# Low parts written over the loaded weight tiles, and loads that wait for TensorE

## The reference

```
for layer in range(2):
    mx, mc = silu(c) @ w_mod[layer] + b_mod[layer], silu(c_ctx) @ w_mod[layer] + b_mod[layer]
    hx, hc = modulate(rmsnorm(x), mx), modulate(rmsnorm(ctx), mc)
    # layer 0: GLA heads and SSD heads, scanned both ways;  layer 1: bidirectional mLSTM
    f = features(h @ w_in)
    x = x + mx[2] * (f @ w_out)
    x = x + mx[5] * ((silu(h @ w1) * (h @ w3)) @ w2)        # h normed and modulated again
return rmsnorm(x)
```

## Time and profile before

| what | us |
|---|---|
| median of 3 runs | 2714.57 (2714.4 to 2721.69) |
| profiled execution, its own time | 2722.84 |
| span of the profiled execution | 2721.1 |
| TensorE busy | 2430.7 |
| VectorE busy | 1483.2 |
| GpSimd busy | 1090.8 |
| mean granted clock of TensorE | 0.934 of full |

### The profile page before, as it was taken

How to read it: one execution, slowest core, us unless ns; L and a number is a source line. 1 busy time by engine, 2 the same in 40 slices (tenths; PEclk the granted TensorE clock), 3 DMA queues, 4 the chain that set the end, 5 groups by cost and what they waited for, 6 DMA issues and landing times.

```text
span 2721.1 us, 33407 instructions
## 1 busy us (share of the span) xinstructions
PE 2430.7 (89%) x11967; PEld 1896.6 (70%) x11967; DVE 1483.2 (55%) x2465; ACT 640.8 (24%) x1041; POOL 1090.8 (40%) x822
## 2 busy tenths in 40 slices
PE   6999999988568899999999898797877968899997
PEld 2878888877226788888888687655444636788886
DVE  3695668683676468877876456203465264322223
ACT  2203434533773311000000321102212021210001
POOL 2443334413672244434354454233000402666663
PEclk9999999989778899999999899898987979899998
DMA  6853334335240124344444254263122211233331
GB/s 241 246 163 105 103 109 129 108 125 165 84 115 24 47 78 124 109 113 119 112 121 102 62 144 154 105 218 119 57 72 78 62 43 39 85 93 100 93 91 49
DMA packets 392114, 292.90 MB, mean 108 GB/s; under 512 B 31330, under 2 KB 351260, under 8 KB 391996
## 3 DMA queue, kind: packets, MB, share of 16 engines
q1 hardware_dynamic: 333452, 201.22, 25.5%
q10 hardware_dynamic: 58544, 90.10, 9.7%
HBM read 249.50 MB, written 41.78 MB: 107 GB/s over the span
## 4 chain that ended last, share of the span: by engine, by line
PE 54%; DVE 10%; ACT 3%; issue 2%; DMA 1%; ACTq 1%; DVEq 0%
PE PS L800 41%; PE PS L1288 3%; DVE xcr L2003 2%; PE PS L1258 2%; PE PS L1195 2%; ACT nh L1366 1%; PE PS L1221 1%; PE PS L752 1%; DVE xcr L1998 1%; PE PS L746 1%; PE PS L1234 1%; PE PS L809 1%; ACT xcr L1698 1%; DVE mf_acc L1905 0%; DVE mtmp L2456 0%
## 5 line engine op out<-in xcount | busy, mean ns | idle before, releaser
L640 POOL TENSOR_TENSOR w_hi<-w_raw,ones 128x128 fp32r<-128x128 f32 x244 | 150.8, 618 | 1303.8 <-PE PS L800 796.9
L800 PE MATMUL PS<-act_hi,w_hi 128*128 128x512 f32 (+1 forms) x2080 | 642.3, 367 | 32.1 <-DVE act_lo L1962 18.3
L800 PE MATMUL PS<-act_lo,w_hi 128*128 128x512 f32 (+1 forms) x2080 | 624.9, 358 | 0.0
L800 PE MATMUL PS<-act_hi,w_lo 128*128 128x512 f32 (+1 forms) x2080 | 624.8, 358 | 0.0
L643 POOL TENSOR_TENSOR w_lo<-w_raw,w_hi 128x1024 fp32r<-128x1024 f32 (+1 forms) x244 | 598.0, 2451 | 20.4
L800 PEld LDWEIGHTS PS<-act_hi,w_hi 128*128 128x128 f32 x2080 | 345.7, 192 | 94.3 <-issue 31.4
L800 PEld LDWEIGHTS PS<-act_lo,w_hi 128*128 128x128 f32 x2080 | 345.9, 192 | 58.2 <-issue 0.5
L800 PEld LDWEIGHTS PS<-act_hi,w_lo 128*128 128x128 f32 x2080 | 345.1, 191 | 58.9
L1905 DVE SCALAR_TENSOR_TENSOR mf_acc<-mf_ring,cs,mf_acc 128x128 f32<-128x128 f32 x784 | 280.6, 433 | 2.0
L641 POOL TENSOR_SCALAR w_hi<-w_raw 128x896 fp32r<-128x896 f32 (+1 forms) x244 | 245.1, 1004 | 0.0
L2184 DVE SCALAR_TENSOR_TENSOR xT<-PS,modv,xT 128x512 f32<-128x512 f32 (+1 forms) x120 | 75.0, 658 | 266.6 <-PE PS L800 266.5
(11 more groups left out here) (322 smaller groups left out, 3256.4 us busy)
## 6 DMA issues: line engine op xcount, KB each, us to landing
w_raw<-in_ffn_w SPq DMA_DIRECT2D x120, 512.0 KB, 3.9
mf_ring<-in_w_mod SPq DMA_DIRECT2D x56, 512.0 KB, 4.0
w_raw<-in_a_w_in SPq DMA_DIRECT2D x44, 512.0 KB, 5.6
proj<-stage ACTq DMA_DIRECT2D x44, 384.0 KB, 2.7
w_raw<-in_b_w_up SPq DMA_DIRECT2D x32, 512.0 KB, 4.0
m_ring<-in_w_mod SPq DMA_DIRECT2D x12, 1024.0 KB, 9.1
rows<-g_d SPq DMA_DIRECT2D x16, 768.0 KB, 5.0
m_raw<-in_w_mod SPq DMA_DIRECT2D x4, 2048.0 KB, 17.1
```

Source lines behind the costliest of these rows:

```text
L640: pool.tensor_tensor(w_hi[:, s, 0], w_raw[:, s, 0], ones[:], ALU.mult)
L800: last = pe.matmul(slot(s)[:, c0:c1], w[:, s, k, :], x[:, k, c0:c1], start=k == 0 and w is w_hi and x is hi, stop=k == kt - 1 and w is w_lo)
```

## The change

The tile `w_lo` is placed at the address of `w_raw`, so that the subtraction writes over its own input, and 16 KB of each partition are free. A slot can then be loaded only when TensorE has finished the unit in it: the loads wait for `mm_done` where they waited for `w_split`. In the SSD stretch the fourth load of out1 would wait for out0's last unit; it moves behind the rows of head 2.

```
+        w_raw_at = top[0]
         w_raw = sb("w_raw", [P, RING, KD, P])
         w_hi = sb("w_hi", [P, RING, KD, P], F32R)
-        w_lo = sb("w_lo", [P, RING, KD, P], F32R)
+        w_lo = nc.alloc_sbuf_tensor_at("w_lo", [P, RING, KD, P], F32R, offset=w_raw_at)
...
                 def load(r, s, kt=kt, src=src):
-                    sp.wait_ge(w_split, r * RING + (s - RING + 1))
+                    sp.wait_ge(mm_done, r * RING + (s - RING + 1))
                     sp.dma_start(w_raw[:, s, 0:kt], src(r, s)).then_inc(w_in[s], 16)
...
-                        sp.wait_ge(w_split, n - RING + 1)
+                        sp.wait_ge(mm_done, n - RING + 1)
                         sp.dma_start(w_raw[:, n % RING], wk[:, :, col:col + P]).then_inc(w_in[n % RING], 16)
...
                     sp.dma_start(rdiag[:], proj0[C0 + 1]).then_inc(b1_in, 16)
-                    each_ring(sp, n0, RING, load)
+                    for s in range(RING - 1):
+                        load(n0 // RING, s)
                     sp.wait_ge(cb_mm, 6)
                     sp.dma_start(bct[:, 0], proj0[B0 + 1]).then_inc(b1_in, 16)
                     for h in range(2, SSD_HEADS):
                         sp.wait_ge(exp_done, h - 1)
                         load_rows(h)
+                        if h == 2:
+                            load(n0 // RING, RING - 1)
```

## The result

Median 2746.06 us (2743.04 to 2750.84, 4 runs) against 2716.56 us before (2714.4 to 2721.69, 4 runs): ratio 1.0107, 95% interval 1.0085 to 1.0130. The change costs 29 us; the forecast had 2724 with a range to 2738. The runs of the kernel before that were made beside the experiments are more in number and have higher medians, 2717 to 2721 us (single runs from 2710 to 2728).

What follows compares the result with a forecast made beforehand. TensorE, busy for 89% of the span, was taken as the bound, so only its waits count. Terms 8.4 + 2.7 - 4 + 4 - 3 + 0.8 + 0.5 = +9.4 us, laid on the median 2714.57, gave 2724.0 us; range 2706 to 2738.

Steps and rivals of the forecast that it cites:

- what is queued behind the wait on SP: qkv's start: m_ring's first load issued about 30 us later, so TensorE stalls for modulation sums; +8.4 us, bounds +2.3 and +15.
- In place: GpSimd's subtraction writing over its own first input: no cost taken.
- the steady state: Most units: a tile is ready 7.8 us after unit n-4 ends, wanted at 16.3, leaving 8.5 us; no cost.
- The lock elsewhere in qkv: Later splits in qkv relieve the products behind the 5.6 us wait at L834; -4 us, bounds -7.8 and 0.
- Layer 0's feed-forward: Splits against products: up00's start +4 us (bounds -2, +6), other waits at L809 -3 us (bounds -9, +4).
- Groups of three: mout1 and up10, 512 columns: window 6.7 us, need 7.8, so late tiles; +2.7 us in all, bounds 0 and 5.
- norms: Segment ends: later splits free the sum of squares but cover the diagonal; before ffn1 +2.6; sum +0.8 us, bounds -4, +5.
- bct: out0 to the SSD heads: bct loaded only after out0's unit 3 ends, landing at 633 to 635; +0.5 us (0 to 5).
- Price: nothing, some 220 of 244 units: Steady-state units, where TensorE has 8.5 us left before it wants the tile: no cost.
- +9.9: qkv's start: SP term if, by the skill's port rule, the split enters after one VectorE instruction and costs its 3 us.
- the +6.9 of the row at 90.76: qkv's start: SP term if the split waits out VectorE's chain, as a 128-wide GpSimd instruction of 2.69 us did.
- Rival 3: qkv: a split pushes VectorE's set late in ten units, 1 us each, heads start 5 late: 2738 us; chance 0.13.

Runs made afterwards that it cites:

- waits_alone: The kernel after with w_lo given its own memory again, all loads still waiting for mm_done: 2746.82 us, ratio 1.0091.
- mended_dcol: The kernel after with m_ring's first loads ahead, rd's split behind unit 3's, SiLU a unit later in xm, dcol's loads behind qkv's evictions: 2710.02 us, ratio 0.9974.
- rd_early: The kernel before with the remainder's split (rd) moved on GpSimd from behind qkv's last tile to behind unit 7's: 2714.49 us, ratio 0.9980.
- w_rest: The kernel before with the wait for mm_done in every segment but qkv, xm and zm, and the change's SSD load order: 2723.86 us, ratio 1.0013.
- w_xm: The kernel before with the wait for mm_done in the loads of xm and zm alone: 2724.36 us, ratio 1.0014.
- conv_pipe: The kernel before with ScalarE in xm evicting unit j before it applies SiLU to unit j-1: 2708.69 us, ratio 0.9946.

## Why the prediction was wrong

Two terms of the sum failed. The largest, for what is queued behind the wait on SP, had the right mechanism and half the size: +17.1 us for +8.4. And xm, priced at nothing, lost 6.0. Together they are 14.7 us. The loss is 21.5 us by the spans and 25 to 29 by the medians, where +9.4 was forecast; what is over 21.5 no trace here can place.

**In place, and the steady state.** Right. waits_alone loses what the whole change loses, and the slack in up11 is 8.4 us for a forecast 8.5.

**What is queued behind the wait on SP.** The mechanism was the one forecast, the place and the issue time too; the size was not: +17.1 for +8.4, above even its upper bound of +15. Three parts. (a) The landing took 13.4 us for the 9.1 assumed. The page's median was taken because "the queue holds less in front of it", yet the loads of its own stretch had a median of 11.2 us and 14.3 at most. And the queue held little in bytes but much in time: behind the gather of dcol, which no term mentions, SP's loads moved no data until 94.2. Where the gather was taken away (mended_dcol), data moved 1.0 us behind the issue; by that, some 2.4 of the 3.4 us are the gather's (an estimate: this order of the loads was not run without it). Then m_ring shared full engines with weight tiles and three stores of the projections. Issued 0.6 us sooner than forecast, it lands 3.7 later. (b) One split of two at half price was charged, 1.5 us; two whole ones fell on the set, since loads that share full engines land while the set runs: 5.9 us, so 4.4 more. (c) The weight tile of unit 4 itself, forecast to be ready 7.8 us behind the unit's end and in time, was late by 1.7: its load took 8 to 9 us there, behind the gather, and mended_dcol shows 4.0 without it. That also moved TensorE's want of the sums from 101.9 to 103.8, so that the stall is 6.3 + 3.7 + 4.4 - 1.9 = 12.5 us by these parts, and 12.75 measured. The low clock behind the stall, priced 2.1, was 2.5 or so.

**The lock elsewhere in qkv.** -2.5 for -4. Unit 13 gained 4.9 us, but units 8 and 12 lost 1.1 and 1.4, which the forecast did not have; waits of 4.6 us in all stay at L838 behind unit 4. rd_early shows that the named cause was right, because without rd's split in the row the whole wait is gone.

**Layer 0's feed-forward.** +3.0 for +4, and -4.2 for -3, of which -3.6 is the change's: both mechanisms right, and w_rest repeats them.

**Groups of three, norms, bct.** +3.2 for +2.7; +2.4 for +0.8 (the norm before up10 alone has +2.0, as the splits of its first tiles now run into it); +1.7 for +0.5, the load of bct being issued at 642.95, behind the units as said.

**What was left out.** xm was booked under "Price: nothing, some 220 of 244 units", with TensorE's slack as its reason. But the splits have a second customer of their time: VectorE, whose convolution in xm runs 24 us behind and in step with them. This is the step that failed in kind: slack of TensorE for its tiles was taken for slack of all that follows the splits. It cost +6.0 us in the trace, shown by the trace of w_xm alone (+5.9) and, from the other side, by conv_pipe. The wait of 15 us at L1164 stood in the waits of the kernel before, and asking what set it would have led there.

**The shared port.** In the set at 104.97 GpSimd's instructions and VectorE's two-input ones take turns in whole instructions: each of a split's three stretches one product to its own length, the longest to the length of a subtraction:

```profile
L1890 DVE SCALAR_TENSOR_TENSOR m_acc<-m_ring,cs,m_acc x42: 470/477/2556, 105.0 to 134.1; 128x256 f32<-128x256 f32 x42
```

The Trainium skill, page "SBUF — State Buffer", section "SBUF: two separate sides", says the same; by that rule the prediction had +9.9, and it was nearer than the +6.9 of the row at 90.76, though still short for want of the second split. Not every meeting goes so: the row at 132.19 below is again like that at 90.76.

Rival 3 (SP's order costs in every unit) did not happen: behind unit 4, units move by 1 us at two places of qkv. Its time, 2738, was the nearest for another reason.

## What to carry to other kernels

A buffer that is freed later moves more than its own work: list everything that stands behind the new wait in the queue, and price its landing with the queue as it will be then, not with a median: ask which transfers are ahead of it, also on other queues, and whether the engines move any data in that time. Then look at each engine that shares a resource with the moved work: one that runs behind the stream and in step with the moved instructions keeps that step, so a harmless shift of 4 us comes out as 4 us at the next barrier. And a wait that the profile shows before the change is worth asking about for its own sake: two of them here gave 22 us together.

## What the runs showed of the hardware

A GpSimd instruction that meets a running chain of VectorE's sometimes gets in at once and sometimes waits the chain out, with the same two instructions: 0.53 us at 106.03 above, but 2.66 us in the same kernel at

```profile
132.19 2.66 POOL L644 TENSOR_TENSOR w_hi<-w_raw,ones 128x128 fp32r<-128x128 f32 x1 [11.92 <-DMA w_raw<-in_a_w_in]
```

What decides it was not tried. A small gather of single words (dcol) on ScalarE's queue doubled the landing of a 512 KB tile behind it on SP's, 9.2 us for 4.0, and it did so with idle engines: their busy share was 0.04 while the tile's data had not begun to move. What holds the tile back was not tried.
